# A decoder block on one Trainium2 core: gate matmuls of 64 columns, in a burst ahead of four weight tiles, or one by one among the wide matmuls of every second tile

## What is computed

```python
def chunk(xc):                                      # 128 tokens
    q = (xc @ w_q).reshape(TOKEN_CHUNK, PEER_HEADS, 2, half)
    s = jnp.einsum('thpd,hpnd->thpn', q, sub_keys)
    top_s, top_i = lax.top_k(s, PEER_TOPK)
    cand = top_s[:, :, 0, :, None] + top_s[:, :, 1, None, :]
    best_s, best_c = lax.top_k(cand.reshape(TOKEN_CHUNK, PEER_HEADS, 256), PEER_TOPK)
    i1 = jnp.take_along_axis(top_i[:, :, 0], best_c // PEER_TOPK, axis=-1)
    i2 = jnp.take_along_axis(top_i[:, :, 1], best_c % PEER_TOPK, axis=-1)
    e = i1 * PEER_N_KEYS + i2                       # 128 x 128 experts
    gate = jax.nn.softmax(best_s, axis=-1)
    h = jnp.einsum('thkd,td->thk', u_tab[e], xc)
    act = jax.nn.gelu(h, approximate=False) * gate
    return jnp.einsum('thk,thkd->td', act, v_tab[e])
```

## Time and profile before

| | before |
|---|---|
| executions (us) | 1192.87, 1195.76, 1197.58 |
| median | 1195.76 us |
| span of the profiled execution | 1195.7 us |
| TensorE matmul busy | 1175.6 us, 98% |
| VectorE busy | 752.9 us, 63% |
| ScalarE busy | 510.1 us, 43% |
| GpSimd busy | 507.7 us, 42% |
| HBM traffic | 152 GB/s over the span |

### The profile page before, as it was taken

How to read it: one execution, slowest core, us unless ns; L and a number is a source line. 1 busy time by engine, 2 the same in 40 slices (tenths; PEclk the granted TensorE clock), 3 DMA queues, 4 the chain that set the end, 5 groups by cost and what they waited for, 6 DMA issues and landing times.

```text
span 1195.7 us, 21882 instructions
## 1 busy us (share of the span) xinstructions
PE 1175.6 (98%) x7850; PEld 1087.5 (91%) x7850; DVE 752.9 (63%) x1232; ACT 510.1 (43%) x798; POOL 507.7 (42%) x216
## 2 busy tenths in 40 slices
PE   8999999999999899999999999999999999999998
PEld 6998989999999899999999999988888888888887
DVE  5467776530898994544343433677787776767675
ACT  6444666454544445333333233333333333444443
POOL 3644444655567766522322233232233332444442
PEclk8999999999999999998988899898999989999999
DMA  5753344444455354444333433333433333555552
GB/s 200 268 183 124 126 141 159 159 146 173 159 175 174 129 189 176 142 141 140 118 118 115 140 123 123 124 128 135 140 137 126 139 123 126 191 193 193 193 193 106
DMA packets 52258, 181.91 MB, mean 152 GB/s; under 512 B 5851, under 2 KB 9051, under 8 KB 52092
## 3 DMA queue, kind: packets, MB, share of 16 engines
q1 hardware_dynamic: 52220, 181.41, 44.3%
HBM read 177.97 MB, written 3.41 MB: 152 GB/s over the span
## 4 chain that ended last, share of the span: by engine, by line
PE 88%; DVE 10%; issue 1%; ACT 1%; DMA 0%; SPq 0%; ACTq 0%; DVEq 0%
PE bank L1047 41%; PE bank L1319 30%; PE bank L1277 10%; PE bank L1128 2%; DVE lo L322 2%; DVE act L885 1%; PE bank L1057 1%; DVE act L880 1%; PE bank L1141 1%; PE bank L1255 1%; DVE act L887 1%; DVE ohA L962 1%; DVE prob L747 0%; DVE act L861 0%; DVE act L856 0%
## 5 line engine op out<-in xcount | busy, mean ns | idle before, releaser
L322 POOL TENSOR_TENSOR lo<-raw,hi 128x1024 fp32r<-128x1024 f32 x202 | 504.7, 2503 | 673.1 <-ACT hi L309 672.7
L309 ACT CAST hi<-raw 128x1024 fp32r<-128x1024 f32 x332 | 348.1, 1049 | 260.6 <-PE bank L1319 249.5
L1047 PE MATMUL bank<-nrm_hi,hi 128*128 128x256 f32 x1504 | 441.2, 293 | 9.9 <-DVE lo L322 7.7
L1047 PE MATMUL bank<-nrm_lo,hi 128*128 128x256 f32 x1504 | 436.6, 290 | 0.0
L1047 PE MATMUL bank<-nrm_hi,lo 128*128 128x256 f32 x1504 | 436.1, 290 | 0.0
L1047 PEld LDWEIGHTS bank<-nrm_hi,hi 128*128 128x128 f32 x1504 | 300.5, 200 | 15.4 <-issue 10.5
L322 DVE TENSOR_TENSOR lo<-raw,hi 128x1024 fp32r<-128x1024 f32 x130 | 171.4, 1318 | 206.5 <-ACT hi L309 206.1
L1047 PEld LDWEIGHTS bank<-nrm_lo,hi 128*128 128x128 f32 x1504 | 300.5, 200 | 0.1
L1047 PEld LDWEIGHTS bank<-nrm_hi,lo 128*128 128x128 f32 x1504 | 299.9, 199 | 0.0
L982 DVE TENSOR_TENSOR nrm_lo<-act,nrm_hi 128x256 fp32r<-128x256 f32 x128 | 142.2, 1113 | 105.1 <-ACT nrm_hi L597 105.1
L572 ACT ACTIVATE act<-bank 128x256 f32 x128 | 49.2, 384 | 284.8 <-PE bank L1047 284.6
(11 more groups left out here) (172 smaller groups left out, 784.2 us busy)
## 6 DMA issues: line engine op xcount, KB each, us to landing
raw<-u_tiles SPq DMA_DIRECT2D x128, 512.0 KB, 3.3
raw<-v_tiles SPq DMA_DIRECT2D x128, 512.0 KB, 3.2
raw<-front SPq DMA_DIRECT2D x76, 512.0 KB, 3.3
toeplitz<-prob SPq DMA_DIRECT2D x12, 192.0 KB, 4.3
bias<-toeplitz SPq DMA_DIRECT2D x12, 128.0 KB, 4.3
resid<-x_t SPq DMA_DIRECT2D x2, 512.0 KB, 4.7
qk<-sub_keys SPq DMA_DIRECT2D x1, 1024.0 KB, 6.6
y<-act SPq DMA_DIRECT2D x2, 512.0 KB, 2.6
```

Of the source, the lines that this page charges most:

```text
L309: act_e.copy(hi[:, s, :], raw[:, s, :]).then_inc(hi_ready, 1)
L322: eng.tensor_tensor(lo[:, s, :], raw[:, s, :], hi[:, s, :].bitcast(F32), ALU.subtract)\
L1047: ins = pe.matmul(dst, w_[:, s, u * P:(u + 1) * P], x_[:, k, :], start=first and i == 0 and p_ == 0, stop=last and i == n - 1 and p_ == 2)
```

## The change

The 32 gate matmuls of a turn are no longer ahead of its four tiles. Those of group 0 stand in tile 0, those of group 1 in tile 2. In a `u` tile a gate matmul follows each first and each second matmul of the three (16 gates for 24 wide). In a `v` tile two gate matmuls stand ahead of each of the first four wide matmuls and one ahead of each of the other eight. VectorE's `multiply` moves from tiles 0 and 2 to tiles 1 and 3, ahead of `one_hots`. No instruction is added or taken away, and no operand differs.

```diff
@@ gate_body (VectorE)
-                    if j % 2 == 0:
+                    if j % 2 == 1:
                         multiply(half, it, j // 2)
-                    elif not last:
-                        one_hots(half, it, 2 + j // 2)
+                        if not last:
+                            one_hots(half, it, 2 + j // 2)
@@ TensorE
+            def gate_part(half, it, g, r):
+                if r == 0:
+                    pe.wait_ge(spread, it * 4 + (half * GROUPS_N + g) * 2 + 2)
+                q, i = divmod(r, 2)
+                ins = pe.matmul(bank[6 + g][:, q * HALF:(q + 1) * HALF], ohA[:, g, :, q], ohB[:, g, i, :, q],
+                                start=i == 0, stop=i == 1, skip_group_check=True)
+                if r == 2 * TOK - 1:
+                    ins.then_inc(gate_mm, 1)
+            def u_tile(base_i, it, j, gates=False):
                 wait(pe, gelu_done, it * 4 + (base_i + j - 1))
-                ins = product(bank[4 + j % 2][:, 0:T], j, [(k, k) for k in range(KB)], nrm_hi, nrm_lo, U0 + base_i, it, j)
-                ins.then_inc(pe_step, 1)
-            def gates(half, it):
...
+                for k in range(KB):
+                    for p_, (w_, x_) in enumerate(((hi, nrm_hi), (hi, nrm_lo), (lo, nrm_hi))):
+                        ins = pe.matmul(dst, w_[:, j, k * P:(k + 1) * P], x_[:, k, :], start=k == 0 and p_ == 0,
+                                        stop=k == KB - 1 and p_ == 2, skip_group_check=True)
+                        if k == KB - 1 and p_ == 2:
+                            ins.then_inc(pe_step, 1)
+                        elif gates and p_ < 2:
+                            gate_part(0, it, j // 2, 2 * k + p_)
@@ u_and_gates
-                gates(0, it)
                 for j in range(RING):
-                    u_tile(HALF, it, j)
+                    u_tile(HALF, it, j, gates=j % 2 == 0)
@@ v_tile
                         for half in range(2):
+                            for _ in range((2 if c == 0 and a_ is nrm_hi else 1) if gates else 0):
+                                gate_part(1, it, j // 2, done_gates)
+                                done_gates += 1
                             ins = pe.matmul(bank[2 * c + half][:, :], a_[:, j, c * P:(c + 1) * P],
@@ v_and_gates
-                gates(1, it)
                 for j in range(RING):
-                    v_tile(0, it, j)
+                    v_tile(0, it, j, gates=j % 2 == 0)
```

More of the change, by code:

```diff
@@ L1261, in _ @@
                     freed(pe, job)
-            def u_tile(base_i, it, j):
-                wait(pe, gelu_done, it * 4 + (base_i + j - 1))
-                ins = product(bank[4 + j % 2][:, 0:T], j, [(k, k) for k in range(KB)], nrm_hi, nrm_lo, U0 + base_i, it, j)
-                ins.then_inc(pe_step, 1)
-            def gates(half, it):
[L1271 to L1279, removed]
+            def gate_part(half, it, g, r):
[7 more added lines that the diff above has]
+            def u_tile(base_i, it, j, gates=False):
+                wait(pe, gelu_done, it * 4 + (base_i + j - 1))
+                wait_lo(pe, U0 + base_i, it, j)
+                dst = bank[4 + j % 2][:, 0:T]
+                for k in range(KB):
[6 more added lines that the diff above has]
+                            gate_part(0, it, j // 2, 2 * k + p_)
             for j in range(RING):
@@ L1308, in _, with v_tile @@
                 u_and_gates(it)
-            def v_tile(base_i, it, j, stop=False):
+            def v_tile(base_i, it, j, stop=False, gates=False):
                 wait_lo(pe, V0 + base_i, it, j)
                 pe.wait_ge(a_hi, it * 4 + (base_i + j + 1))
+                done_gates = 0
                 for c in range(TC):
```

## The result

Four executions of the changed kernel took 1202.60 to 1209.58 us, median **1206.7 us**, against 1195.67 for the kernel before in the same session: ratio 1.0099, 95% interval 1.0069 to 1.0129. The change makes the kernel slower by 1.0%. The forecast was 1197 us, with a range of 1180 to 1210. The execution whose rows follow took 1202.60 us and is the fastest of the four; its span is 1200.8 us.

A forecast was written before the change was run, and what follows sets the result against it. TensorE was taken to bound the kernel, its clock falling behind gate bursts: 1195.7 - 39.4 (clock) + 38.9 (passages between wides and gates) + 0.8 (idle between stages) + 0.7 (possible clock fall there) = 1196.7, 1197 us; range 1180 to 1210.

The forecast's parts named there:

- slower, at 0.22: Whole kernel: a time above the range of 1180 to 1210 us; chance 0.22.
- the one at 0.58: Whole kernel: a time within the range of 1180 to 1210 us; chance 0.58.
- a late VectorE: Rival, v stage: drawn-out one-hot steps make VectorE late and TensorE stands still, 1212 us; chance 0.07.
- What bounds the kernel, and the clock: Both gate stages: TensorE bounds; its clock falls behind bursts of 32 gates, and spreading them gives back 39.4 us.
- The entries, 0.04 us each: Passages from a wide matmul to a gate, both stages: the gate's weight load lies bare, 896 x 0.04 = 35.8 us.
- Going out of a burst is cheap.: Passages from gate to wide: no surcharge in the u stage, 0.008 us each in the v stage, 3.1 us in all.
- The transition: From u stage to v stage: 1.2 us idle waiting for `nrm_hi`, +0.8 us, and +0.7 for an even chance of one clock fall.
- `multiply` costs nothing: VectorE: `multiply` moved behind a wait for the tile just run; a 5.35 us chain fits into 8.8 us, cost nothing.
- hidden under the wide: Rival, wide to gate: the gate's weights load under the wide after all, so 35.8 us fall away, 1161 us; chance 0.14.
- the second rival: Both gate stages: the clock isn't given back while the passages are paid, 1196.7 + 38.2 = 1235 us; chance 0.05.
- The gate tiles were put at 5.5 and 5.2 us: Sign that the forecast is right: gate tiles of about 5.5 us in the u stage and 5.2 in the v stage.

The follow-up runs named there:

- the bursts of 16: Kernel before, its burst of 32 gates cut into 16 ahead of tile 0 and 16 ahead of tile 2, VectorE's order as before: 1158.1 us, ratio 0.9677.
- the run with float32r gates: The change with the gates' operands replaced by float32r data of the same shape, gates not computed: 1145.4 us, ratio 0.9579.
- the version that computes: Kernel before with one-hot matrices laid out key innermost and gates 16 ahead of tile 0 and 16 ahead of tile 2, everything computed: 1104.5 us, ratio 0.9223.

## Why the prediction came out as it did

- *The outcome.* The result lies in the range of 1180 to 1210, but outside the forecast's own spread (1189 to 1205), and it is 11 us above the kernel before, where the text takes 6 us as no change. So the case came that it called slower, at 0.22, and not the one at 0.58. The upper end of the range was made for a late VectorE, which did not come; that the range holds the result is in part luck.
- *What bounds the kernel, and the clock.* Right. The stretches at 0.50 are gone, and the bursts of 16 put the gain at 38.2 us, or 39.5 without their entries, against 39.4 read. The matmuls of 128 columns in the earlier trace rows, which the rows and the text call transposes, are products of the queries with the sub keys (L1255). What it draws from them, that they left the clock at 1.00, isn't touched by that.
- *The entries, 0.04 us each.* Right, in size (0.159 to 0.163) and place. The runs give its cause more exactly: the late start belongs to an fp16 load behind a float32r matmul, and what stands out of it is the part that reading 16 bytes apart adds.
- *"Going out of a burst is cheap."* **This step failed.** It was read behind a burst of 32 and carried over to an exit behind a single gate, as no row of before shows one. Behind one gate it costs 0.015 us more, 768 times, 11.5 us: the gate's late load holds up the wide's. The text had both halves of this, the late load of the gate and the time of a wide's load ("takes 0.13 us until its own successor may load"), but didn't put one behind the other. It bounded the entry from both sides and gave the exit no bound. The forecast (1197) and the result (1206.7) differ by 9.7. From the medians the gates cost 31.9 us more than before, where 35.8 were priced (3.3 of that difference had been counted with the clock, as a gate in a burst takes 0.122 us and the bursts had 32 entries), and the wides behind them 15, where 3.1 were. By stage: the u stage was forecast at -0.4 us and came to +5.6, off by the 6 us that the text named as its limit; the v stage was forecast at +1.5 and came to +4.7.
- *The transition.* The idle time was 1.16 us for 1.2. In the traced execution no fall came, 0.7 us less than priced; the other three executions have no trace.
- *`multiply` costs nothing.* Right: 0.3 us of waits, as before, and 0.9998 for that edit in the kernel before. Of the one-hot steps `ohB` was drawn out to about 2.9 us, as costed, in 32 of 64 groups; the other two steps hardly ever were (3 of 128).
- *The rivals.* The load isn't hidden under the wide: 1161 us did not come. The Trainium skill's statement ("TensorE: Matmul & The Clock Gate", the step-by-step section of its Part 2), that the next weights load while the present matmul runs, agrees with the run with float32r gates (605.05 and 605.04), and not with fp16 gates. The clock stayed at 1.00, and VectorE wasn't late. The 38.2 us of the second rival are derived nowhere (with the 39.4 it would be 1236 us); nothing hangs on it.

The gate tiles were put at 5.5 and 5.2 us. From the groups above it is 8 x 0.705 = 5.64, and 4 x 0.51 + 8 x 0.41 = 5.32.

## What to carry to other kernels

Small matmuls should stand in short bursts: long enough that few loads lie bare, short enough that the clock isn't lost (here 16 gates of 0.12 us and not 32). Before spreading work among other work, count the passages, and price the way in and the way out for the new size of group, not for the old one. And ask first why the small matmul costs what it does: its reads were worth more here than any order of the instructions (107 us against the kernel before where the gates aren't computed, and 54 against the bursts of 16 alone in the version that computes; the order alone gave 38). Work moved from one engine to another can hold the first one up: look at how long its steps take while the other one works.

## What the runs showed of the hardware beyond that

- A matmul of 64 fp16 columns takes 0.12 us with its moving operand read 16 bytes apart, 0.06 with only the stationary one so, 0.029 with neither. The Trainium skill ("SBUF — State Buffer", "Door 1: The DMA port swizzle") says that each access which crosses to a new line of 16 bytes pays a penalty; the order of these three agrees.
- The clock fell behind bursts of 32 such gates of 3.8 us in which TensorE was never idle, and not behind 16 of them. With neighbouring reads, 32 gates take 0.95 us, and it stayed at 1.00 through both stages but for one fall at their border. With only the moving operand near they take 1.9 us, and it never fell there. So it isn't the number of gates alone.
- A float32 weight load behind a matmul of 0.03 us lies bare: 0.199 us from gate to a wide of 0.12, and 0.312 to one of 0.227.
- A VectorE step with two inputs in SBUF stands still while GpSimd subtracts (0.42 and 2.62 us, 1.22 and 2.91 us). The Trainium skill (same page, "SBUF: two separate sides") tells of a lock on a shared pair of ports; the trace agrees.
- Between two weight loads behind a single gate, the gate's and the wide's, 0.111 to 0.112 us lie from end to end, in the change as with near reads. Why an fp16 load doesn't start under a float32r matmul, and a float32r load does under an fp16 one, stays open.
